# Loading every ring matrix as two transfers of 1 MB, each half of an expert's slot freed and refilled by itself

## What is computed

```python
def hierarchical_moe(x, w_router_group, w_router_expert, w_gate, w_up, w_down):
    ...
    for e in range(N_EXPERTS):                      # 32
        h = jax.nn.silu(t @ w_gate[e]) * (t @ w_up[e])   # w_gate, w_up: (32, 1024, 512)
        out = out + combine[:, e:e + 1] * (h @ w_down[e])  # w_down: (32, 512, 1024)
    return out.reshape(b, s, d)
```

## Time and profile before

| | |
|---|---|
| median of 3 runs | 1088.04 us (1086.84 to 1089.54) |
| the profiled execution | 1090.25 us, its span 1088.5 us |
| TensorE busy | 819.8 us (75% of the span) |
| bytes moved by DMA | 438.58 MB, mean 403 GB/s |
| mean granted clock of TensorE | 0.902 of full speed |

### The profile page before, as it was taken

One profiled execution on the slowest core, in us unless ns is written; L12 is line 12 of the kernel. 1 busy time (PEld: TensorE's weight loads), 2 busy tenths in 40 slices (PEclk: granted clock), 3 DMA queues, 4 the chain that ended last, 5 costly groups with the idle time before them and its releaser, 6 DMA issues.

```text
span 1088.5 us, 30531 instructions
## 1 busy us (share of the span) xinstructions
PE 819.8 (75%) x13955; PEld 640.7 (59%) x13956; DVE 321.6 (30%) x803; ACT 190.5 (17%) x364; POOL 10.3 (1%) x32
## 2 busy tenths in 40 slices
PE   8999996757667675776899998875767666676865
PEld 7887774545445454554699976654545444454643
DVE  5666531111111111111177644211111111111112
ACT  6565210000000000000163321100000000000002
POOL 3000000000000000000000000000000000000000
PEclk9999999898988889798899999989898888979889
DMA  9976999999999999999999599999999999999995
GB/s 341 414 261 252 402 426 428 429 428 428 429 428 429 428 429 428 429 428 425 413 387 407 220 376 427 428 429 428 429 428 429 428 429 426 431 427 430 426 425 232
DMA packets 47020, 438.58 MB, mean 403 GB/s; under 512 B 5600, under 2 KB 7164, under 8 KB 22140
## 3 DMA queue, kind: packets, MB, share of 16 engines
q1 hardware_dynamic: 44972, 436.54, 96.1%
q10 hardware_dynamic: 2000, 1.32, 0.4%
HBM read 436.80 MB, written 1.05 MB: 402 GB/s over the span
## 4 chain that ended last, share of the span: by engine, by line
DMA 63%; PE 29%; DVE 4%; issue 3%; ACT 1%; SPq 0%; ACTq 0%; DVEq 0%
DMA ring<-in_w_up 58%; PE psum L1419 8%; PE psum L1270 8%; PE psum L1301 4%; DMA ring<-in_w_down 3%; PE psum L1428 2%; PE psum L1285 2%; PE psum L1436 1%; PE psum L1448 1%; DMA ring<-in_even_w_in 1%; DVE ring_halves L771 1%; ACT ring_halves L529 0%; PE psum L1442 0%; PE psum L1234 0%; PE psum L1215 0%
## 5 line engine op out<-in xcount | busy, mean ns | idle before, releaser
L1419 PE MATMUL psum<-ring,m 128*32 128x128 f32 x7936 | 314.4, 324 | 228.4 <-DMA ring<-in_w_gate 106.4
L1419 PEld LDWEIGHTS psum<-ring,m 128*32 128x32 f32 x7936 | 273.6, 131 | 275.8 <-DMA ring<-in_w_up 109.7
L1121 DVE TENSOR_TENSOR m<-psum,m 128x128 f32<-128x128 f32 x64 | 18.6, 291 | 577.3 <-ACT m L674 577.1
L1428 PE MATMUL psum<-ring,m 128*32 128x256 f32 x1984 | 120.1, 380 | 14.0 <-DMA ring<-in_w_down 10.7
L674 ACT ACTIVATE m<-psum 128x128 f32<-128x128 f32 x64 | 17.8, 278 | 530.5 <-PE psum L1419 530.5
L1270 PE MATMUL psum<-scr_halves,ring_halves 128*128 128x256 f32 x768 | 106.3, 285 | 3.6 <-DVE ring_halves L771 3.6
L1270 PEld LDWEIGHTS psum<-scr_halves,ring_halves 128*128 128x128 f32 x768 | 100.6, 194 | 4.1 <-DVE ring_halves L771 4.0
L1428 PEld LDWEIGHTS psum<-ring,m 128*32 128x32 f32 x1984 | 65.6, 110 | 60.1 <-issue 18.3
L1436 PE MATMUL psum<-m 32*128 32x256 f32 x1056 | 82.4, 426 | 3.0 <-DVE m L1126 1.1
L771 DVE TENSOR_TENSOR ring_halves<-ring,ring_halves 128x2048 fp32r<-128x2048 f32 (+1 forms) x34 | 68.2, 2037 | 12.5 <-ACT ring_halves L529 12.5
L1448 PE MATMUL psum<-x,m 128*32 128x256 f32 x1024 | 69.4, 385 | 3.1 <-DVE m L1090 2.3
(11 more groups left out here) (194 smaller groups left out, 507.6 us busy)
## 6 DMA issues: line engine op xcount, KB each, us to landing
ring<-in_w_gate SPq DMA_DIRECT2D x62, 2048.0 KB, 40.5
ring<-in_w_up SPq DMA_DIRECT2D x62, 2048.0 KB, 40.7
ring<-in_w_down SPq DMA_DIRECT2D x60, 2048.0 KB, 41.1
ring<-in_odd_w_in SPq DMA_DIRECT2D x5, 2048.0 KB, 19.8
ring<-in_even_w_in SPq DMA_DIRECT2D x4, 2048.0 KB, 14.2
ring<-in_even_w_out SPq DMA_DIRECT2D x2, 2048.0 KB, 19.2
spare<-in_w_down SPq DMA_DIRECT2D x2, 2048.0 KB, 22.9
ring<-in_w_down SPq DMA_DIRECT2D x8, 512.0 KB, 36.2
```

The source lines that it names most:

```text
L1419: last = pe.matmul(GU[CAP * part:CAP * (part + 1), lo:lo + FP], block_of(k), w_of(k)[:, FP * part:FP * (part + 1)], start=k == 0, stop=k = ...
L1428: last = pe.matmul(YB[CAP * part:CAP * (part + 1), 0:DP], hhT[:, CAP * f:CAP * (f + 1)], w[:, f, DP * part:DP * (part + 1)], start=f == 0, ...
```

## The change

Every ring transfer is cut into two: the first half of the partition's run and the second, 1 MB each. Both add 16 to the slot's semaphore, and `wait_landed` asks for 32 for each matrix, so a reader still waits for both. For slots that hold an expert's matrix, TensorE reports on `half_used[mat]` when it has done the first half of the matrix (k = 3 of 8 for gate and up, f = 1 of 4 for down), and SP waits for that before the first transfer, and for the old semaphore before the second. For a slot that held a mixer's matrix both waits are the old one. `load_quarters`, `load_early`, `load_spare` and the last down are as before. Some semaphores of small loads are merged, so that the seven are now four.

```diff
+        half_used = [sem(f"half_used{mat}") for mat in range(3)]
-        smalls_loaded = [sem(f"smalls_loaded{i}") for i in range(7)]
+        smalls_loaded = [sem(f"smalls_loaded{i}") for i in range(4)]
...
+        def half_used_up(n):
+
+            for l in range(2):
+                if L_MOE[l] <= n < L_MOE[l] + PER_MOE:
+                    n -= L_MOE[l]
+                    if n >= 3 * EARLY:
+                        n += 3
+                    e, mat = divmod(n, 3)
+                    return half_used[mat], after(l, e)
+            return used_up(n)
...
-            eng.wait_ge(landed[n % RING], (turns + (n // RING + 1 - apart)) * 16)
+            eng.wait_ge(landed[n % RING], (turns + (n // RING + 1 - apart)) * 32)
...
-            def load(n, src, dst):
-                sp.dma_start(dst, src).then_inc(landed[n % RING], 16)
+            def load_half(n, src, dst, h):
+                half = dst.shape[1] // 2
+                part = slice(half * h, half * (h + 1))
+                sp.dma_start(dst[:, part], src[:, part]).then_inc(landed[n % RING], 16)
...
-                if former >= 0:
-                    sp.wait_ge(*used_up(former))
-                load(n, src, dst)
+                for h in range(2):
+                    if former >= 0:
+                        sp.wait_ge(*(half_used_up, used_up)[h](former))
+                    load_half(n, src, dst, h)
...
-                    sp.wait_ge(used, after(l, e - TRI))
-                    load(n, matrix(l, e, mat), buffer(n, mat))
+                    for h, freed in enumerate((half_used[mat], used)):
+                        sp.wait_ge(freed, after(l, e - TRI))
+                        load_half(n, matrix(l, e, mat), buffer(n, mat), h)
...
-            for i in (5, 6):
-                pool.wait_ge(smalls_loaded[i], 32)
+            pool.wait_ge(smalls_loaded[3], 64)
...
+                    if half and k == HK - 1:
+                        last.then_inc(half, 1)
...
+                    if half and f == 1:
+                        last.then_inc(half, 1)
```

More of the change, by code:

```diff
@@ L422, in small_loads @@
                 sp.dma_start(rows[0:24, :], odd_conv_w[0].rearrange("c (j p) -> (c j) p", p=P)).then_inc(smalls_loaded[2], 16)
-                sp.dma_start(rows[24:28, :], gmlp_v_gain[0].rearrange("(j a) d -> j (a d)", a=2)).then_inc(smalls_loaded[3], 16)
+                sp.dma_start(rows[24:28, :], gmlp_v_gain[0].rearrange("(j a) d -> j (a d)", a=2)).then_inc(smalls_loaded[2], 16)
                 for l in range(2):
-                    sp.dma_start(rgraw[:, l], router_group[l].rearrange("(p k) g -> p k g", k=K)).then_inc(smalls_loaded[5], 16)
-                    sp.dma_start(reraw[:, l], router_expert[l].rearrange("g (p k) e -> p g k e", k=K)).then_inc(smalls_loaded[6], 16)
+                    sp.dma_start(rgraw[:, l], router_group[l].rearrange("(p k) g -> p k g", k=K)).then_inc(smalls_loaded[3], 16)
+                    sp.dma_start(reraw[:, l], router_expert[l].rearrange("g (p k) e -> p g k e", k=K)).then_inc(smalls_loaded[3], 16)
             for t in range(TT):
@@ L1321, in even @@
                 channels(L + 1, (6, 7), k_ready)
-                pe.wait_ge(smalls_loaded[2], 16)
-                pe.wait_ge(smalls_loaded[3], 16)
+                pe.wait_ge(smalls_loaded[2], 32)
                 pe.transpose(bank[4][:, 0:28], rows[:, :], ident[0:28, 0:28]).then_inc(cols_turned, 1)
@@ L1414, in odd, with gate_up @@
                 project_out(L + 6, 1, lambda j: pe.wait_ge(mix_lo_made, j // 2 + 1))
-            def gate_up(w_of, block_of, lo):
+            def gate_up(w_of, block_of, lo, half=None):
                 for k in range(K):
@@ L1420, in gate_up, with down @@
                                          w_of(k)[:, FP * part:FP * (part + 1)], start=k == 0, stop=k == K - 1)
+                    if half and k == HK - 1:
+                        last.then_inc(half, 1)
                 return last
-            def down(w, wait_part=None):
+            def down(w, wait_part=None, half=None):
                 for f in range(NP):
@@ L1469, in expert @@
                         w_of = lambda k: wide(n + mat)[:, k, :]
-                    gate_up(w_of, block_of, FP * mat).then_inc(used, 1)
+                    gate_up(w_of, block_of, FP * mat, half_used[mat]).then_inc(used, 1)
                     if mat == (0 if rest and e == NE - 1 else 1):
@@ L1482, in expert @@
                     pe.wait_ge(spare_landed, 16 * (l + 1))
-                    down(spare).then_inc(y_ready, 1)
+                    down(spare, half=half_used[2]).then_inc(y_ready, 1)
                 elif rest and e == NE - 1:
-                    down(tall(n + 2), lambda f: pe.wait_ge(last_landed[f], 16 * (l + 1))).then_inc(y_ready, 1)
+                    down(tall(n + 2), lambda f: pe.wait_ge(last_landed[f], 16 * (l + 1)), half_used[2]).then_inc(y_ready, 1)
                 else:
                     wait_landed(pe, n + 2, turns)
-                    down(tall(n + 2)).then_inc(y_ready, 1)
+                    down(tall(n + 2), half=half_used[2]).then_inc(y_ready, 1)
             def moe(l):
```

## The result

The changed kernel took 1097.93 us (median of 4 runs, 1097.53 to 1098.16) beside 1088.53 us for the kernel before on the same chip, a ratio of 1.0086 (95% interval 1.0075 to 1.0098), 9.4 us slower. Forecast were 1101.6 us, in a range of 1090 to 1109. The profiled execution took 1097.53 us, its span 1095.8. Some executions were disturbed and slow (one of the kernel before took 1180 us, one of another kernel 4058 us, four of the seven of the kernel cut by partitions over 1760 us), and all ratios here leave them out.

A forecast was written before the change was run, and what follows sets the result against it. The prediction took DMA transfers in the expert stages as the bound. Shorter rows cost 170 x 0.08 = 13.6 us, other terms about 0, so 1088.04 + 13.6 = 1101.6 us, range 1090 to 1109.

The forecast's parts named there:

- What bounds the kernel: Expert stages: transfers are the limit, TensorE has slack; two saturated stretches, 832 us together at 428 GB/s, last bytes over rate.
- Earlier release: Ring slots: SP may issue a first half some 2 us sooner, but it only stands longer in the queue; 0 us.
- Depth of the queue: Ring queue: about eight halves stand in it, issue to landing falls from 41 to about 20 us, no loss.
- Shorter rows: Expert ring matrices: 8 KB rows make 16 packets instead of 8 for each engine, costing 0.08 us a matrix.
- the bounds: Cost of 8 KB rows for a matrix: at least nothing, at most 0.11 us with completions; 1088.0 to 1106.7 us.
- the interpolation from 2, 4 and 16 KB rows: Rates of other stretches give 7.9 to 9.5 ns for each added packet, 0.063 to 0.076 us for a matrix.
- the second set of completions: Each matrix cut in two has 32 completions instead of 16, costing up to 0.01 us.
- 170 matrices and 13.6 us: Both layers: 85 whole matrices each are cut in two, 170 x 0.08 = 13.6 us slower.
- each lands after the one before it in one unbroken queue: All 170 matrices: TensorE waits at the queue's end, so the delay adds up through both layers, 13.6 us.
- The rate stays: Rival for the expert stages: 8 KB rows already reach the ceiling, time unchanged at 1088 us; chance 0.12.
- The ring's latency is the bound: Rival for the saturated stretches: earlier first halves shorten each 44.0 us turn by 1 us, 19 us, 1069 us; chance 0.05.
- A fixed cost of a transfer: Rival: each of 170 additional transfers adds an unhidden cost beyond packets, 24 us, 1112 us; chance 0.07 with dry queue.

The follow-up runs named there:

- the kernel cut by partitions: Against the kernel before: every ring matrix in two 1 MB transfers, partitions 0 to 63 and 64 to 127, rows whole, no early release; ratio 1.590.
- The shallow kernel: Against the kernel before: whole transfers, but SP waits for an expert two later, so about two matrices stand in the queue; 1115.55 us, ratio 1.0253.
- halves for the mixers: Against the kernel before: only the mixers' 13 matrices are cut in halves, expert matrices stay whole; 1088.51 us, ratio 1.0002.

## Why the prediction was right, and where its sum was off

*What bounds the kernel* was right: the rate went down by 1.6% at an unchanged DMA share, and the two stretches grew by 7.2 and 5.9 us (below). The nine matrices of a turn now take 9 x 4.972 = 44.75 us; 44.7 was forecast.

*Earlier release, 0 us*: right, by the run without it.

*Depth of the queue, 0 us*: right for this change. But the size was off: a half lands 26.4 us after its issue at 2.49 us each, so ten or so stand ahead of it, where the forecast put down eight and 20 us. The shallow kernel shows where the cover ends: not in the steady part, even at two matrices, but where TensorE comes late out of a mixer.

*Shorter rows, 0.08 us for a matrix*: right, 0.079 measured. Of the bounds, nothing and 0.11, the interpolation from 2, 4 and 16 KB rows was the one to trust. Whole 2 MB transfers with 8 KB rows give (4.960 - 4.893)/8 = 8.4 ns for an added packet, inside the 7.9 to 9.5 read from the other stretches. For the second set of completions I had allowed 0.01 us; the windows leave at most 0.012, the stages below show none.

*170 matrices and 13.6 us*: the price holds, but the sum over the whole kernel was too large. By the measured 0.079 us it is still 13.4 us, and the medians say 9.4, 11.0 for the same kernel run again, and 10.4 without the early release. Where the rest went can be read from the landings. B0 and B1 are SP's bursts that open the two expert stages (gate and down are their first two matrices), D0 and D1 the landings of that down, E0 and E1 the landings of the last quarter of the stage's last down. Lengths in us:

| profile | B0 to D0 | D0 to E0 | E0 to B1 | B1 to D1 | D1 to E1 |
|---|---|---|---|---|---|
| before | 14.9 | 417.4 | 99.5 | 14.9 | 419.3 |
| before, again | 14.9 | 417.2 | 99.1 | 13.5 | 418.8 |
| halves for the mixers | 14.7 | 417.7 | 99.1 | 15.1 | 419.2 |
| changed | 13.8 | 424.3 | 98.6 | 13.7 | 424.6 |
| changed, again | 13.5 | 425.1 | 99.4 | 14.4 | 425.2 |
| changed, no early release | 13.6 | 424.4 | 98.6 | 14.2 | 425.1 |
| whole, rows of 8 KB | 14.6 | 424.9 | 97.4 | 14.1 | 425.3 |

Between D and E, 83 whole matrices land in each stage, for which 83 x 0.079 = 6.6 us were due. From the first three rows to the next three the means grow by 7.2 and 5.9 us, 13.1 together, just what 166 matrices at 0.079 us make. What comes back lies outside: 1.2 us from B0 to D0, 0.4 from B1 to D1 and 0.3 between the stages. That leaves some 11 us. Of what comes back, only the 1.2 us at B0 are well clear of the spread: the profiles of one kernel differ by up to 0.3 us there, but by 1.6 us from B1 to D1.

So the step that was too coarse is "each lands after the one before it in one unbroken queue", for all 170. The prediction also read the chain of waits as landings all the way from 172 to 1077 us. It has them only in the two steady parts; from 482 to 679 us the chain runs in the main through work of TensorE, as in these pieces of it:

```profile
481.98 1.47 PE psum L1436 x16
542.64 1.98 PE psum L1428 x32
563.21 57.59 PE psum L1270 x480
```

The second of them is the last down of layer 0. In this profile TensorE came to it without a wait for a landing, and in the other two of the first three rows it waited 0.2 and 0.4 us. The delay still adds up through layer 0, but with next to nothing in hand.

At B0 the queue has run nearly dry, and there the halves come sooner, not later. Landings of the ring transfers issued from 109.5 to 111.6 us, first of the kernel before in its second profile (gate, then down), then of the changed kernel (two halves of each):

```profile
DMA to landing us min/median/max: 10.1/12.3/14.6
```

```profile
DMA to landing us min/median/max: 5.0/9.5/12.4
```

The down matrix is issued at 110.44 and complete at 125.0 us, 14.9 after B0. Its second half is issued at about 111.1 and complete at 123.5, 13.8 after B0. In 109.5 to 125 us DMA moves 395 GB/s in the changed kernel and 375 in the other, so there were idle moments to fill. It isn't the early release, and whole transfers with the same short rows take 14.6 us, so at B0 the gain goes with the cut into two transfers. What makes it stays open.

The last row also warns against the third decimal of a window. By its rate in 200 to 470 us (0.067 us) the kernel with whole transfers should be 1.0 us shorter than the changed one from D to E in each stage; it isn't.

The sum was also set against one execution, at 1090.25 us, with the clock's accident in it, and its 2.2 us were then rightly taken off again for the median.

*Rivals.* "The rate stays" fell to 422 GB/s; the landings that allowed it were read to 0.1 us, and the effect is 0.08. "The ring's latency is the bound" fell with the sign. "A fixed cost of a transfer" fell to at most 0.012 us, by the kernel with whole transfers and 8 KB rows. The Trainium skill's rule of at least 1 MiB in a transfer ("DMA: Bandwidth & Descriptors", section "Rules for kernel authors") decides nothing here: the change keeps to it and loses, and a whole 2 MB transfer with 8 KB rows loses as much.

No version beat the kernel before. What was left to gain by the halves was an earlier start, and that is worth nothing behind a queue.

## What to carry to other kernels

Where a chain of waits runs from landing to release to issue to landing, compare the time from issue to landing with the time that one transfer moves: if it is many times as long, the loop is a queue, and an earlier release buys nothing. In such a kernel the rate goes by the length of the contiguous row in a partition, not by the size of the transfer (2 MB or 1 MB here), so count the packets before you split one; stretches of the same trace with other rows give the price in advance. Judge the depth of a queue where its consumer comes late out of another stage, not in the steady part.

## What the runs showed of the hardware

Price of a row: 429, 423, 410 and 387 GB/s with rows of 16, 8, 4 and 2 KB (the third with four transfers for a matrix, the last from the mixer's stretch), close to one line of 8 to 9.5 ns for each added packet.

Pairs of transfers to 64 of the 128 partitions each moved 217 GB/s through layer 0, half the rate, and up to 375 GB/s late in layer 1, with all engines busy throughout.

SP's issue is held when enough stands in the queue. With about ten halves ahead (8 packets for each engine apiece, 26.4 us at 2.49 us) an issue took 2.1 to 3.3 us, and with eight whole matrices (also 8 packets) 0.33. Whole matrices with 8 KB rows, 16 packets for each engine, held it with between six and seven ahead (32.5 us from issue to landing at 4.96 us). Here is SP's timeline in that kernel, one transfer in each row, 4.6 us and more for an issue; the limit can't be a number of transfers alone, and it isn't known here what it is.

```profile
208.25 4.68 SPq L333 DMA_DIRECT2D ring<-in_w_gate  x1
213.03 4.57 SPq L333 DMA_DIRECT2D ring<-in_w_up  x1
```

The granted clock was at the lower level (1.2 GHz) for 3.4 us of one execution, from 25.4 us on, in a stretch bound by TensorE, and at 2.4 GHz there in another execution of the same kernel. The next stage began 1.3 us later for it.
